# One slab of query weights, loaded in fifteen pieces of unequal height

## What is computed

```
h = rmsnorm(x) ;  one projection gives attention, index, retention inputs
x += concat(sparse_attention(h), retention(h)) @ w_out
h2 = rmsnorm(x)
q = (h2 @ w_query).reshape(T, 8 heads, 2, 128)      # w_query is 1024 x 2048
per head: scores against keys1, keys2; top 16 of each; top 16 of the 256 sums
          -> 16 expert rows out of 16384
act = gelu(u[expert] . h2) * softmax gate ;  x += sum act * v[expert]
y = rmsnorm(x)
```

## Time and profile before

| | |
|---|---|
| median of 3 runs | 1158.07 us (1157.69 to 1158.08) |
| the profiled execution's own time | 1156.52 us |
| its span, first to last instruction | 1154.5 us |
| PE busy | 873.4 us (76%) |
| DVE busy | 816.6 us (71%) |
| POOL busy | 544.4 us (47%) |
| ACT busy | 448.7 us (39%) |
| moved by transfers | 458.68 MB, mean 397 GB/s |
| share of that by POOL's queue (the gathers) | 402.68 MB |
| share of that by SP's queue | 54.97 MB |

### The profile page before, as it was taken

One profiled execution on the slowest core, in us unless ns is written; L12 is line 12 of the kernel. 1 busy time (PEld: TensorE's weight loads), 2 busy tenths in 40 slices (PEclk: granted clock), 3 DMA queues, 4 the chain that ended last, 5 costly groups with the idle time before them and its releaser, 6 DMA issues.

```text
span 1154.5 us, 12183 instructions
## 1 busy us (share of the span) xinstructions
PE 873.4 (76%) x3735; PEld 396.8 (34%) x3740; DVE 816.6 (71%) x2123; ACT 448.7 (39%) x1413; POOL 544.4 (47%) x437
## 2 busy tenths in 40 slices
PE   8999988997897957765766769587666756656566
PEld 6748743443333424232233333133222212211111
DVE  2325887876687889996867785757887777777544
ACT  2121444343444434433554663343333333333334
POOL 0002445553554645554553563545574555556442
PEclk9999999999998879787899898798988698887769
DMA  9902999999999999999999999999999999999995
GB/s 377 402 1 72 423 425 425 426 426 430 423 390 425 422 429 425 382 424 425 427 426 424 425 427 427 427 426 428 426 424 426 427 426 427 427 423 418 426 426 226
DMA packets 67079, 458.68 MB, mean 397 GB/s; under 512 B 8387, under 2 KB 10179, under 8 KB 15686
## 3 DMA queue, kind: packets, MB, share of 16 engines
q0 software_dynamic: 55888, 402.68, 83.2%
q1 hardware_dynamic: 10982, 54.97, 11.7%
q10 hardware_dynamic: 144, 0.26, 0.1%
HBM read 453.59 MB, written 3.24 MB: 396 GB/s over the span
## 4 chain that ended last, share of the span: by engine, by line
DMA 43%; PE 25%; DVE 17%; POOL 6%; issue 5%; ACT 3%; SPq 0%; POOLq 0%; DVEq 0%
DMA rows<-in_uv,ids 32%; PE ps L596 25%; DMA wt<-in_uv,ids 8%; DVE rows L2007 7%; POOL rows L535 3%; POOL work L518 2%; DMA rows<-in_w_qi 1%; DMA wt<-in_uv,last_ids 1%; DMA wt<-in_w_q 1%; DVE wt L2007 1%; DVE top L1596 1%; ACT work L1227 1%; DVE wt L1600 1%; ACT wt L1227 1%; POOL wt L535 1%
## 5 line engine op out<-in xcount | busy, mean ns | idle before, releaser
L535 POOL DMA_INDIRECT rows<-in_uv,ids x352 | 407.5, 1158 | 447.6 <-PE ps L596 360.4
L596 PE MATMUL ps<-rows,work 128*64 128x512 f32 x1416 | 419.5, 722 | 236.0 <-ACT work L1227 235.8
L2007 DVE CUSTOM_DVE_ANT_0 rows<-rows,wt 128x1024 f32<-128x1024 f32 x226 | 276.9, 1226 | 150.7 <-DMA rows<-in_uv,ids 147.5
L1227 ACT ACTIVATE zact<-zdot 128x1 f32<-128x1 f32 x354 | 71.5, 202 | 510.1 <-DVE zdot L2007 509.9
L596 PEld LDWEIGHTS ps<-rows,work 128*64 128x64 f32 x1416 | 97.4, 154 | 475.2 <-ACT work L1227 329.4
L596 PE MATMUL ps<-wt 128*128 128x128 f32 (+6 forms) x719 | 195.6, 478 | 27.8 <-ACT wt L1227 26.0
L2007 DVE CUSTOM_DVE_ANT_0 rows<-rows,masks 128x1024 f32<-128x1024 f32 x128 | 157.4, 1232 | 55.7 <-DMA rows<-in_uv,ids 53.1
L596 PEld LDWEIGHTS ps<-wt 128*128 128x128 f32 (+2 forms) x724 | 97.9, 187 | 105.9 <-issue 59.3
L1227 ACT ACTIVATE work<-pair,wgt 128x64 f32<-128x64 f32 x354 | 123.1, 348 | 11.5
L1227 ACT ACTIVATE wgt<-zact,gates 128x1 f32<-128x1 f32 x354 | 104.3, 295 | 11.5
L596 PEld LDWEIGHTS ps<-work,wt 128*128 128x128 f32 (+1 forms) x664 | 85.7, 204 | 55.1 <-issue 55.1
(11 more groups left out here) (175 smaller groups left out, 744.8 us busy)
## 6 DMA issues: line engine op xcount, KB each, us to landing
wt<-in_w_q SPq DMA_DIRECT2D x8, 2048.0 KB, 12.2
rows<-in_uv,ids POOLq DMA_INDIRECT x352, 13.9
rows<-in_w_out SPq DMA_DIRECT2D x2, 2048.0 KB, 31.8
wt<-in_w_out SPq DMA_DIRECT2D x2, 2048.0 KB, 11.3
wt<-in_ckv SPq DMA_DIRECT2D x16, 256.0 KB, 10.8
x<-in_x SPq DMA_DIRECT2D x5, 512.0 KB, 9.0
rows<-in_w_qi SPq DMA_DIRECT2D x1, 2048.0 KB, 13.4
wt<-in_w_qa SPq DMA_DIRECT2D x1, 2048.0 KB, 11.3
```

The lines of the kernel that those rows point to most:

```text
L535: pool.indirect_dma_start(row[s], None, a["uv"], bass.IndirectOffsetOnAxis(ap=ids[:, own(n // KP).start + n % KP:own(n // KP).start + n % ...
L596: return nc.tensor.matmul(out, lhsT, rhs, start=start, stop=stop)
L1227: return nc.scalar.activation(*args, **kw)
L2007: V.tensor_tensor_reduce(row[s][:, 0:D], row[s][:, 0:D], h2r[t][:, n % 2, :], 1.0, 0.0, ALU.mult, ALU.add, zdots[s]).then_inc(dotted, 1)
```

## The change

Load k = 7 is issued as fifteen transfers of 15, 14, 13, 12, 11, 10, 9, 9, 8, 7, 6, 5, 4, 3 and 2 partitions (128 together), one below the other, each with its own increment of 16 on the same semaphore. PE's wait for it asks for 15 x 16. Nothing else is changed.

```diff
+        STAIRS = (15, 14, 13, 12, 11, 10, 9, 9, 8, 7, 6, 5, 4, 3, 2)
...
                 dst = wt[:, 0 if k < 7 else k - 4, :] if k else at(rowf, SLOT, SLOT)
-                sp.dma_start(dst, a[f"w_q{Q_LOADS[k]}"]).then_inc(q_in[max(0, k - 6)], 16)
+                if k == 7:
+                    p = 0
+                    for n in STAIRS:
+                        sp.dma_start(dst[p:p + n, :], a[f"w_q{Q_LOADS[k]}"][p:p + n, :]).then_inc(q_in[1], 16)
+                        p += n
+                else:
+                    sp.dma_start(dst, a[f"w_q{Q_LOADS[k]}"]).then_inc(q_in[max(0, k - 6)], 16)
...
-                        pe.wait_ge(q_in[max(0, k - 6)], 16 * (k + 1 if k < 7 else 1))
+                        pe.wait_ge(q_in[max(0, k - 6)], 16 * (k + 1 if k < 7 else len(STAIRS) if k == 7 else 1))
```

## The result

| | before | after |
|---|---|---|
| median of the runs | 1157.88 us (1155.4 to 1158.36, 6 runs) | 1182.74 us (1181.09 to 1184.17, 6 runs) |
| the profiled execution | 1156.52 us | 1181.73 us |
| its span | 1154.5 us | 1179.7 us |

The ratio is 1.0219, with a 95% interval from 1.0205 to 1.0234: 24.9 us slower. The forecast was +7.6 and 1165.7; the sign was right, the size is three times that, and the time lies above the range. All lines of the changed kernel behind the change stand seven lower, so PE's L596 is L603 and DVE's L2007 is L2014.

The account below looks back on a forecast made before the run. All 16 DMA engines were taken as always having work queued, with one late engine setting the end. The busiest engines' +13.7 less 6.1 hidden gave +7.6 on the median of 1158.07: 1165.7 us, range 1155.8 to 1178.

Parts of the forecast that it names:

- Issue, landing, PE's wait: SP's 15 issues from 703.55 us take 7.5 us; slab lands long before PE's unit 20 at 875.15; cost 0.
- Shares and the narrow factor: Slab load: first two engines carry 15 rows instead of 8, and rows to few partitions take longer; together +13.7 us.
- I take the factor of the row, 2.02: Slab rows cost 1.24 us instead of 0.615, a factor measured on the h2 copies to 64 partitions.
- Rival 4: Narrower transfers are worse again: 106 GB/s at 16 partitions, slab takes 19.8 us; +13.1 us, 1171.2; chance 0.15.
- I count nothing beyond the busiest engine's own time: Gathers around 703 to 740 us: slow engines keep their backlog, quick ones run dry on slack; no extra cost.
- What hides some of it: At the program's end, the first two engines' 6.1 us lead over the late engine is subtracted: +13.7 becomes +7.6.
- 1: Slab load: narrow destinations cost nothing and the late engine is relieved; -1.8 us, 1156.3, up to 3 faster; chance 0.25.
- 2: Slab load: narrow destinations cost nothing, but the late engine is among the first few; up to +4.3, 1162.4; chance 0.06.
- 5: Slab load: rows are spread evenly whatever the height, at full rate, so nothing happens; 1158; chance 0.05.
- Rival 3: Slab load at the forecast's cost, with the late engine among the first: +13.7 without slack, 1171.8; chance 0.09.
- the combination of 3 and 4: Rival 3 and Rival 4 both holding for the slab load; left out of the range, given no size or chance.
- the rate below 300 GB/s after 704 us: Sign: from 704 to about 735 us the DMA rate falls below 426 GB/s, to 300 or less in parts.

Follow-up runs that it names:

- the last pair: Kernel before with load k = 7 as one 64-partition transfer plus eight of 8, every fourth partition; the two runs exchange the halves: 1162.11 and 1169.92 us.
- two_loaded: Kernel before with load k = 7 as one transfer of 112 partitions and eight of two partitions lying 8 apart: 1164.86 us, ratio 1.0063.
- late_first8: Kernel before with load k = 8 asked for at about 893 us, as 16 transfers of 8 partitions on the first eight engines: 1172.14 us.
- s8_halves: Kernel before with load k = 7 as 16 half-row transfers of 16 partitions, each at every eighth partition: 1164.21 us, ratio 1.0056.

## Why the prediction was wrong

- **Issue, landing, PE's wait: right.** 5.88 us on SP where 7.5 were worked out, hidden as said. PE first uses the slab at 902.30 us; its waits for the query weights come to 4.1 us in the whole program, against 6.4 before.
- **Shares and the narrow factor: right in kind, too small.** The step "I take the factor of the row, 2.02" gave 13.7 us for both. The form alone costs 18.3 more than a whole slab. The factor holds at 64 and 32 partitions (210 and 223 GB/s) and fails below: 16 neighbours ran at 133 GB/s, and a row among 14 took 2 us, not 1.24. So the failed term is the price of a row. Rival 4 had this mechanism, at 106 GB/s and a chance of 0.15; its price for the slab, 19.8 us against 15.8 measured for eight transfers of 16, was nearer than the forecast's 9.9. **+4.6 us.**
- **"I count nothing beyond the busiest engine's own time": wrong.** I had let the slow engines keep their backlog and the quick ones run dry at no cost. The share did not fall in the windows from 710 to 750 us (0.98 to 1.06) while the rate was 154 to 213 GB/s: the gathers' own rows were slowed with the slab's. Beside the gathers the form costs 24.9, alone 18.3. **+6.6 us.** That a foreign row holds up the owner of its partitions fits the last pair and is not shown; how the 6.6 divide among the engines is open.
- **"What hides some of it", -6.1: wrong.** The step that failed is the subtraction: that the first two engines "set the new end", 6.1 us less than their extra time, while the late one is "relieved or little loaded". Four places of the same form cost 24.4 to 28.1 us, never less than the 18.3 of the form alone. At the end one engine is still alone for 3 us, where it was for nearly 6 (for 1 in two_loaded). That looks like a lead drawn on, and the end still came 24.9 us later. Most likely the late engine was itself held up with the gathers; which engine is last, and so whether that is the whole reason, stays open. Booked here as **+6.1 us**.

The three add up: 4.6 + 6.6 + 6.1 = 17.3, on 7.6 is 24.9. This is book-keeping on medians, each good to a us or so, and it adds up by construction. Only the first term was measured by itself. The other two are 12.7 together: if the lead did hide 6.1, what the form does to the gathers costs 12.7, and no run separates the two. The set of alone costs against costs beside the gathers says the same for the other forms:

| form | alone, over the whole slab | beside the gathers |
|---|---|---|
| 2 x 64 | +3.7 | +6.1 |
| 4 x 32 | +3.1 | +5.4 |
| 8 x 16 neighbours | +9.5 | +14.4 |
| 8 x 16, every eighth | +3.2 | +7.3 |
| 9 neighbouring | +10.7 | +17.1 |
| 9, every ninth | +1.8 | +4.4 |
| 112 and eight pairs | +6.6 | +7.3 |
| 15 unequal (the change) | +18.3 | +24.9 |
| 16 unequal, every ninth | +6.8 | +12.7 |
| 16 x 8, first eight engines (late_first8) | +7.2 | +15.6 |
| 8 x 16 in half rows (s8_halves) | +4.6 | +6.7 |

In every row the second number is larger, by 0.7 to 8.4 us, and none shows the 6.1 us of relief that the prediction counted on. Forms that SP probably paces when alone (every ninth, half rows) need less of the engines than the first number says.

Of the rivals, 1, 2 and 5 fell with the rate: it dropped to 154. Rival 3 (the late engine among the loaded) gave 1171.8 by leaving the lead out, and with rival 4's price and no lead the sum would have been 14.9 + 4.3 = +19.2, 1177.3; the range's upper end of 1178 was drawn there, and "the combination of 3 and 4" was named as left out. The gathers' 6.6 were in no case at all.

Of the signs named ahead, the rate below 300 GB/s after 704 us and DVE's new waits of 10 us (9.80 and 12.91) came. So did the products' delay at the end (25.2 us), and the shorter stretch at 0.06 with a second engine (0.12 to 0.13) before it: the sign came, and the time that the lead was to bring did not. Quick engines running dry shows only behind the slow stretch, and little: 0.94 from 750 to 760 us, 0.96 from 760 to 770. The landing of the narrow transfers can't be read: the profile gives no time for them.

## What to carry to other kernels

Where all 16 engines always have work, price a transfer by the bytes that are not moved beside it: sum the gap between the usual rate and the rate in the windows, whatever the share says, since a share of 1 at half the rate hid the whole loss here. Load a tile in one transfer to all 128 partitions; pieces of 64 or 32 already cost 5 to 6 us for 2 MB here, pieces of 16 neighbours 14, and unequal ones 25. Don't subtract a lead that engines have over the last one from a delay that may fall on the last one too: in two_loaded the surplus of 4.3 us is less than the lead of nearly 6, and the kernel was 7.3 us slower.

## What had not been expected of the hardware

- 64 and 32 neighbouring partitions are about equally slow (210 and 223 GB/s, against 426), and 16 are much slower (133).
- Two patterns of transfers with the same widths, heights and shares differ by 7.8 us by which half of the partitions the first engines write (1162.11 and 1169.92).
- The records' busy share stays at 1 while engines are held up: 154 GB/s at 1.00 from 730 to 740 us.
- Doubling the number of transfers at the same bytes per engine costs nothing that can be measured beside the gathers (1164.80 and 1164.21), though SP issues for 10.39 us in place of 5.33.
- late_first8's 10.7 us beyond its surplus of 4.9 stay open; alone its form costs 7.2 us over the whole slab. By theory F its 16 transfers go mostly to foreign partitions, but no run held that fixed with its shares.
